# The final norm of a two-block transformer kernel: even tiles scaled on ScalarE and multiplied by the norm's weights on GpSimd, odd tiles on VectorE

## The chip, the cores and the metric

The kernel runs on one core of one Trainium2 chip. The metric is the device time of one execution in microseconds (us), as the median of several runs.

## What is computed

Two transformer blocks in float32 over 1024 tokens with 1024 features: the first has latent attention and a gated side input, the second a gated delta rule and a retention, followed by a mixture of 64 experts of which each token uses two. The change lies in the last lines of it, the sum of the two expert results of a token and the norm of the whole:

```python
def rms_norm(x, w):
    xf = x.astype(jnp.float32)
    y = xf * lax.rsqrt(jnp.mean(xf * xf, axis=-1, keepdims=True) + EPS)
    return (y * w.astype(jnp.float32)).astype(x.dtype)
...
        h2 = rms_norm(x, ffn_norm[l])
        x = x + hierarchical_moe(h2, w_router_group[l], w_router_expert[l],
                                 w_gate[l], w_up[l], w_down[l])
    return rms_norm(x, final_norm)
```

## The kernel before, in words

The program is written for each engine by hand, stage after stage, with semaphores between the engines. The tokens are cut into T = 8 tiles of 128 partitions, so a tile is 128x1024 floats (512 KB). The stages are: the projections, the attention, the output of the first block, the projections of the second block, its recurrence over tiles (the `L2042` to `L2316` lines), the experts, and the last stage, which the change touches. Nothing of the expert stage has to be known but that it leaves the two results of each token, y0 and y1, in the DRAM tensor `y_d`.

The last stage is four functions, one for each of the engines SyncE, VectorE, ScalarE and GpSimd.

- `f_sp` loads the residual tiles `xf` and the weights of the final norm `fn2` (copied to all partitions) while the experts still run, and after the last scatter loads `yf` from `y_d` in four transfers of two tiles each (L2752). Then it waits for the tiles in order, 0 to 7, and stores each to `out` (L2756). One transfer is issued as soon as its tile is done, and never ahead of a lower tile.
- `f_dve` adds in two instructions (L2767), y0 and then y1, each times its per-token weight, into `xf`. Each addition waits for its predecessor. Two tiles later it finishes the tile (`last`, L2773) with one scalar_tensor_tensor: `xf` times the per-token factor times `fn2`. It writes the tile in place.
- `f_act` squares the tile and sums the squares (L2783, an ACTIVATE and the reading of its accumulator), when y1 is in.
- `f_pool` makes the factor from the sum in two instructions on a 128x1 column: `ms` (L2788, scale and add) and `rs` (L2790, to the power -0.5). They are in order by tile.

`Count` is a helper for semaphores: each name that is "done" raises it by one, and `wait(engine, name, t)` waits until the name of tile t has been done. All are counted in the program order of one engine. Below, `rs(3)` is the L2790 instruction of tile 3, and so on; `add y0`, `add y1` are the two of L2767.

The order on VectorE is therefore add(0), add(1), add(2), last(0), add(3), last(1), and so on until add(7), last(5), last(6), last(7). Other lines that the prediction's steps name are of the recurrence stage: L2303 is a 128x1024 multiplication on GpSimd, L2042 and L2124 are 128x1024 multiplications on VectorE, L2242, L2246, L2248 are 128x512 multiplications on GpSimd, L2094 is a 128x512 addition on VectorE, L2307 is a power on GpSimd. L1018 is a Copy on ScalarE with a per-token factor over 128x1024.

Of the kernel before, what the change touches and what calls it, by code (L numbers as in the profile page):

```python
# [11 lines left out]
ALU = mybir.AluOpType  # L12
ACT = mybir.ActivationFunctionType
# [84 lines left out]
def build(nc, A, out):  # L98

    ctx = ExitStack()  # L100
    with ctx:  # L101
        def sem(name):
            return ctx.enter_context(nc.semaphore(name))
# [3 lines left out]
        def sb(name, shape, off, dt=F32):  # L107
            return nc.alloc_sbuf_tensor_at(name, shape, dt, offset=base_off + off)
# [8 lines left out]
        def wait(eng, semaphore, value):  # L117

            if not isinstance(value, int):
                eng.wait_ge(semaphore, value)
                if eng.engine in (mybir.EngineType.Pool, mybir.EngineType.SP):
                    eng.sem_inc(s_alone, 1)
            elif value > 0:
                eng.wait_ge(semaphore, value)
# [1467 lines left out]
        for s in STEPS:  # L1594
            for name in ENDING.get(s, ORDER):
                t = s - LAG[name[0]]
# [43 lines left out]
        pool_l = Count("l_pool", "ms rs"); act_l = Count("l_act", "sq"); dve_l = Count("l_dve", "hn")  # L1640
# [735 lines left out]
        def m_full(eng, b, n):  # L2376

            wait(eng, bank_full[b], n + base_m[b])
# [350 lines left out]
        xf = sb("xf", [P, T, D], SLOT[2])  # L2729
# [3 lines left out]
        fn2 = sb("fn2", [P, D], SLOT[2] + 32 * KB)  # L2733
        s_fn2 = sem("fn2_in")
        dve_f = Count("f_dve", "y0 y1", after=dve_n); dve_out = Count("f_out", "out", after=dve_a)
        act_f = Count("f_act", "sq", after=act_n)
        pool_f = Count("f_pool", "ms rs", after=pool_a)
        s_out = sem("out_stored")
        ssF, msF, rsF = ([stat_d[:, 8 * i + p:8 * i + p + 1] for p in range(4)] for i in range(3))

        def f_sp(sp):
            for q in range(2):
                wait(sp, s_x4st[q], 16 * T // 2)
            m_full(sp, 2, N_FIX - 2)
            for t in range(T):
                sp.dma_start(xf[:, t, :], x4_d[t * P:(t + 1) * P, :]).then_inc(s_xf, 16)
            m_full(sp, 5, N_FIX - 2)
            sp.dma_start(fn2[:, :], A["final_norm_2"].partition_broadcast(P)).then_inc(s_fn2, 16)
            wait(sp, s_phase, PH_M)
            for i in range(T // 2):  # L2750
                t = 2 * i
                sp.dma_start(yf[t // 4][:, t % 4:t % 4 + 2, :, :],  # L2752
                             y_d[t * 2 * P:(t + 2) * 2 * P, :].rearrange("(a p k) n -> p a k n", a=2, k=2)).then_inc(s_yf[i], 16)
            for t in range(T):
                dve_out.wait(sp, "out", t)
                sp.dma_start(out[0, t * P:(t + 1) * P, :], xf[:, t, :]).then_inc(s_out, 16)  # L2756
            wait(sp, s_out, 16 * T)

        def f_dve(v):
            v.wait_ge(s_fn2, 16)  # L2760
            v.wait_ge(s_wt, 5)
            v.wait_ge(s_xf, 16 * T)

            def add(t):
                v.wait_ge(s_yf[t // 2], 16)  # L2765
                for k in range(2):
                    dve_f.done(v.scalar_tensor_tensor(xf[:, t, :], yf[t // 4][:, t % 4, k, :], w_tok[:, k, t:t + 1], xf[:, t, :],  # L2767
                                                      ALU.mult, ALU.add), f"y{k}")
                    dve_f.wait(v, f"y{k}", t)

            def last(t):
                pool_f.wait(v, "rs", t)
                dve_out.done(v.scalar_tensor_tensor(xf[:, t, :], xf[:, t, :], rsF[t % 4], fn2[:, :], ALU.mult, ALU.mult), "out")  # L2773
            for t in range(T + 2):
                if t < T:
                    add(t)
                if t >= 2:
                    last(t - 2)

        def f_act(act):  # L2780
            for t in range(T):
                dve_f.wait(act, "y1", t)
                act_f.done(act.activation(yf[t // 4][:, t % 4, 0, :], xf[:, t, :], ACT.Square, accum_out=ssF[t % 4]), "sq")  # L2783

        def f_pool(pool):
            for t in range(T):
                act_f.wait(pool, "sq", t)
                pool_f.done(pool.tensor_scalar(msF[t % 4], ssF[t % 4], 1.0 / D, EPS, ALU.mult, ALU.add), "ms")  # L2788
                pool_f.wait(pool, "ms", t)
                pool_f.done(pool.tensor_tensor(rsF[t % 4], msF[t % 4], neghalf[:, 0:1], ALU.pow), "rs")  # L2790

        block = ctx.enter_context(nc.Block())

        @block.sync
        def _(sp):
            setup_sp(sp)
            a_sp(sp)
            att_sp(sp)
            b_sp(sp)
            c_sp(sp)  # L2800
            d0_sp(sp)
            d_sp(sp)
            moe_sp(sp)
            f_sp(sp)
# [12 lines left out]
        @block.scalar  # L2817
        def _(act):
            setup_act(act)
            a_act(act)  # L2820
            att_act(act)
            b_act(act)
            c_act(act)
            d0_act(act)
            d_act(act)
            moe_act(act)
            f_act(act)

        @block.vector
        def _(v):  # L2830
            setup_dve(v)
            a_dve(v)
            att_dve(v)
            b_dve(v)
            c_dve(v)
            d0_dve(v)
            d_dve(v)
            moe_dve(v)
            f_dve(v)

        @block.gpsimd
        def _(pool):
            a_pool(pool)
            phase_a_end(pool)
            att_pool(pool)
            b_pool(pool)
            b_end(pool)
            c_pool(pool)
            d_pool(pool)
            moe_pool(pool)  # L2850
            f_pool(pool)
# [21 lines left out]
```

## Time and profile before

| | |
|---|---|
| median of 3 runs | 2313.5 us (2313.23 to 2316.52) |
| the profiled execution, its own time | 2314.25 us |
| its span in the trace | 2312.5 us |
| VectorE busy in the whole span | 771.1 us (33%) |
| ScalarE busy | 620.4 us (27%) |
| GpSimd busy | 497.4 us (22%) |
| TensorE busy | 2029.7 us (88%) |

The trace has the time from 0 to 2312.5 us; the execution's own time has 1.75 us around it. DVE is VectorE, ACT ScalarE, POOL GpSimd, PE TensorE, SP SyncE; a letter q behind an engine is its sequencer. Busy time includes the time in which a started instruction is held by something, and this is why one and the same instruction can have different durations.

### The profile page before, as it was taken

The page shows a single profiled execution, that of the slowest core. Times are in us where ns is not written, and L with a number is a line of the kernel's source. Part 1 is how long each engine was busy: PE and PEld are TensorE (multiplying, and loading weights), DVE is VectorE, ACT ScalarE, POOL GpSimd, SP SyncE. Part 2 cuts the span into 40 slices and gives each one's busy share as a digit, 9 for nine tenths or more (in the row PEclk, how much of TensorE's full clock was granted, in tenths as well). Part 3 has the DMA queues.
Part 4 walks back from the last instruction along what each step waited for, and adds up shares of the span by engine and source line. Part 5 has one row for each costly group of instructions (what it writes and reads, how often), then busy time and mean ns, then how long its engine had stood idle before and what let it go on. Part 6 is the DMA issues. An engine that isn't in the chain of part 4 may idle for free. (4 is left out here: it accounts for less than half of the span.)

```text
span 2312.5 us, 30382 instructions
## 1 busy us (share of the span) xinstructions
PE 2029.7 (88%) x11531; PEld 1297.3 (56%) x11531; DVE 771.1 (33%) x1407; ACT 620.4 (27%) x1358; POOL 497.4 (22%) x559
## 2 busy tenths in 40 slices
PE   7999996999989999999999679989987887878780
PEld 4555553666667876687888467666653322323220
DVE  1110112555553344343111155677642111111115
ACT  2222223555542334233211243233211111111111
POOL 1122113200002111000010177656501111111103
PEclk9999997999999999999999789999987998999995
DMA  6122116212122114342232422211185999999995
GB/s 250 46 58 78 45 37 209 52 32 56 28 97 97 54 37 107 73 86 69 73 100 82 166 75 87 86 65 62 50 344 225 424 425 425 423 422 421 419 372 233
DMA packets 98423, 375.17 MB, mean 162 GB/s; under 512 B 16949, under 2 KB 33402, under 8 KB 71418
## 3 DMA queue, kind: packets, MB, share of 16 engines
q1 hardware_dynamic: 77370, 314.67, 36.7%
q0 software_dynamic: 19776, 54.55, 6.8%
q10 hardware_dynamic: 1152, 4.19, 0.4%
q8 instruction: 89, 1.46, 0.3%
q14 instruction: 36, 0.29, 0.0%
HBM read 323.04 MB, written 67.11 MB: 169 GB/s over the span
## 5 line engine op out<-in xcount | busy, mean ns | idle before, releaser
L2425 PE MATMUL ps<-w_gu,rows_t 128*64 128x512 f32 x1024 | 263.8, 675 | 63.1 <-DMA w_gu<-w_up 61.5
L2425 PEld LDWEIGHTS ps<-w_gu,rows_t 128*64 128x64 f32 x1024 | 79.9, 154 | 224.1 <-issue 158.5
L390 PE MATMUL ps<-w_u,x_t 128*128 128x512 f32 (+2 forms) x512 | 185.6, 524 | 4.3 <-DVE x_t L460 4.3
L626 PE MATMUL ps<-k_s,q_s 96*128 96x512 f32 (+3 forms) x384 | 154.5, 514 | 19.1 <-issue 19.1
L390 PEld LDWEIGHTS ps<-w_u,x_t 128*128 128x128 f32 x512 | 98.3, 192 | 90.1 <-issue 62.6
L863 PE MATMUL ps<-tk_lo,h_hi 128*128 128x512 f32 x320 | 125.5, 392 | 3.0 <-DVE tk_lo L855 3.0
L2683 POOL DMA_INDIRECT y_d<-y_out,asg_i x32 | 32.1, 1004 | 438.6 <-DVE y_out L2509 424.1
L863 PE MATMUL ps<-tk_hi,h_lo 128*128 128x512 f32 x320 | 125.1, 391 | 0.0
L863 PE MATMUL ps<-tk_hi,h_hi 128*128 128x512 f32 x320 | 125.1, 391 | 0.0
L2500 DVE TENSOR_TENSOR act_s<-act_g,ps 128x256 f32<-128x256 f32 x32 | 13.5, 421 | 334.7 <-ACT act_g L2491 334.7
L1898 PE MATMUL ps<-w_o,mix_t 128*128 128x512 f32 x256 | 124.9, 617 | 0.0
L2443 PE MATMUL ps<-w_d,act_tt 128*64 128x512 f32 x512 | 116.9, 598 | 0.5 <-issue 0.5
L755 ACT ACTIVATE prob<-ps,stats 128x256 f32<-128x256 f32 (+7 forms) x128 | 94.6, 739 | 36.6 <-DVE stats L717 35.6
L2491 ACT ACTIVATE act_g<-ps 128x256 f32<-128x256 f32 x32 | 12.3, 383 | 332.7 <-PE ps L2425 332.7
L626 PEld LDWEIGHTS ps<-k_s,q_s 96*128 96x128 f32 x384 | 64.0, 194 | 61.7 <-issue 61.2
L717 DVE TENSOR_REDUCE stats<-ps 128x1 f32<-128x256 f32 (+7 forms) x128 | 97.0, 758 | 4.7 <-DVE ps L715 0.3
L636 PEld LDWEIGHTS ps<-consts,prob 128*128 128x128 f32 x576 | 69.1, 142 | 48.7 <-issue 39.7
L636 PE MATMUL ps<-consts,prob 128*128 128x128 f32 x576 | 85.9, 276 | 11.7 <-DVE prob_t L693 10.4
L863 PE MATMUL ps<-h_lo,ch_hi 128*128 128x512 f32 x192 | 77.3, 403 | 8.9 <-DVE ch_lo L855 5.6
L650 PE MATMUL ps<-prob_t,v_all 128*64 128x128 f32 x1152 | 77.7, 280 | 1.1 <-ACT prob_t L691 0.8
L1139 POOL TENSOR_TENSOR o_s<-sz_in,rinv 128x1024 f32<-128x1024 f32 x8 | 15.8, 1977 | 288.2 <-DVE rinv L721 256.0
L863 PE MATMUL ps<-h_hi,ch_lo 128*128 128x512 f32 x192 | 76.0, 396 | 0.0
(399 smaller groups left out, 3695.9 us busy)
## 6 DMA issues: line engine op xcount, KB each, us to landing
w_gu<-w_gate SPq DMA_DIRECT2D x64, 1024.0 KB, 21.5
w_gu<-w_up SPq DMA_DIRECT2D x64, 1024.0 KB, 24.9
w_d<-w_down SPq DMA_DIRECT2D x64, 1024.0 KB, 18.9
w_tk<-w_in SPq DMA_DIRECT2D x5, 2048.0 KB, 12.1
proj_d<-tok_o POOLq DMA_DIRECT2D x40, 256.0 KB, 2.3
tk_in<-proj_d SPq DMA_DIRECT2D x8, 1280.0 KB, 5.9
yf<-y_d SPq DMA_DIRECT2D x4, 2048.0 KB, 14.4
q_d<-q_feat POOLq DMA_DIRECT2D x8, 768.0 KB, 6.6
```

Source lines behind the costliest of these rows:

```text
L390: mm = pe.matmul(b[:, 0:cn], x_t[p][:, k, :], w_u[:, k, c0:c0 + cn], start=(k == 0), stop=(k == KD - 1))
L626: mm = pe.matmul(ps[:, b, 0:cn], q_s[p][:, a, i * P:(i + 1) * P], k_s[p][:, a, g * BANK:g * BANK + cn], start=True, stop=True)
L636: mm = pe.transpose(b[:, (k - 4 * g) * P:(k - 4 * g + 1) * P], prob[j % 2][:, k * P:(k + 1) * P], ident)
L650: mm = pe.matmul(ps[half, b, (i % 4) * P:(i % 4 + 1) * P], v_all[:, k, bass.ds(u * (2 * VD) + a * VD, VD)], prob_t[(2 * i + a) % 4][:, k, ...
L717: v.tensor_reduce(nmax[j % 4], flat[:, 0:n], AX.X, ALU.max, negate=True).then_inc(s_max, 1)
L755: act.activation(prob[j % 2][:, 0:n], flat[:, 0:n], ACT.Exp, bias=nmax[j % 4], accum_out=rsum[p][:, j // 2, j % 2:j % 2 + 1]).then_inc(s_e ...
L863: mm = pe.matmul(out_, a, b_, start=(n == 0), stop=(n == 3 * len(pairs) - 1))
L1139: pool.tensor_tensor(o_s[:, :].rearrange("p (h n) -> p h n", h=HEADS), sz_in[t % 2][:, :].rearrange("p (h n) -> p h n", h=HEADS), bc(rinv[ ...
L1898: mm = pe.matmul(b, mix_t[:, k, :], w_o2[:, k, j * BANK:(j + 1) * BANK], start=(k == 0), stop=(k == KD - 1))
L2425: mm = pe.matmul(ps[half, 2, :].rearrange("p (g n) -> p g n", g=2), rows_t[:, k, half], w_gu[q][:, h, :, k, :], start=(k == 0), stop=(k == ...
L2443: mm = pe.matmul(ps[half, 4 + j, :], act_tt[:, k, half], w_d[q][:, h, k, j * BANK:(j + 1) * BANK], start=(k == 0), stop=(k == 1))
L2683: pool.indirect_dma_start(out=y_d, out_offset=bass.IndirectOffsetOnAxis(ap=idx, axis=0), in_=y_out[q][:, :], in_offset=None, bounds_check= ...
```

## The change

In the last stage the finishing of the even tiles 0, 2, 4 and 6 is taken from VectorE. ScalarE multiplies the tile by its per-token factor, in place, in the iteration of the next odd tile and ahead of that tile's square. GpSimd multiplies it by `fn2`, in place, behind `rs` of the next odd tile. SyncE waits for GpSimd or VectorE by the parity of the tile. GpSimd also waits once for the load of `fn2`. The odd tiles are finished on VectorE at the place where they were.

```diff
+        act_s2 = Count("f_act_scaled", "scaled", after=act_l); pool_out = Count("f_pool_out", "out", after=pool_l)
...
             for t in range(T):
-                dve_out.wait(sp, "out", t)
+                (dve_out if t % 2 else pool_out).wait(sp, "out", t // 2)
                 sp.dma_start(out[0, t * P:(t + 1) * P, :], xf[:, t, :]).then_inc(s_out, 16)
...
             for t in range(T + 2):
                 if t < T:
                     add(t)
-                if t >= 2:
+                if t >= 2 and t % 2:
                     last(t - 2)
 
         def f_act(act):
+            def scaled(t):
+                pool_f.wait(act, "rs", t)
+                act_s2.done(act.activation(xf[:, t, :], xf[:, t, :], ACT.Copy, scale=rsF[t % 4]), "scaled")
+
             for t in range(T):
+                if t % 2:
+                    scaled(t - 1)
                 dve_f.wait(act, "y1", t)
                 act_f.done(act.activation(yf[t // 4][:, t % 4, 0, :], xf[:, t, :], ACT.Square, accum_out=ssF[t % 4]), "sq")
 
         def f_pool(pool):
+            pool.wait_ge(s_fn2, 16)
             for t in range(T):
                 act_f.wait(pool, "sq", t)
                 pool_f.done(pool.tensor_scalar(msF[t % 4], ssF[t % 4], 1.0 / D, EPS, ALU.mult, ALU.add), "ms")
                 pool_f.wait(pool, "ms", t)
                 pool_f.done(pool.tensor_tensor(rsF[t % 4], msF[t % 4], neghalf[:, 0:1], ALU.pow), "rs")
+                if t % 2:
+                    act_s2.wait(pool, "scaled", t // 2)
+                    pool_out.done(pool.tensor_tensor(xf[:, t - 1, :], xf[:, t - 1, :], fn2[:, :], ALU.mult), "out")
```

## Rows read from the trace of the kernel before

**Rows 1.** The page: the span, and the lines of the chain that ended last

```profile
span 2312.5 us, 30382 instructions
...
DVE xf L2767 1%; DMA yf<-y_d 0%; DVE xf L2773 0%; POOL stat_d L2788 0%; ACT yf L2783 0%; DMA y_d<-y_out,asg_i 0%; POOLq L2385 0%; POOLq L101 0%; ACTq L101 0%; POOLq L2386 0%; DVEq L2765 0%; POOLq L2725 0%
```

**Rows 2.** The chain that ended last, in order of time: start, us, what

```profile
2273.36 1.30 DVE xf L2767
...
2285.12 1.28 DVE xf L2773
2286.41 1.21 DVE xf L2767
...
2300.47 1.06 ACT yf L2783
...
2303.66 1.28 DVE xf L2773
```

**Rows 3.** Groups by line and form from 2270 us on: busy us, mean ns, idle before

```profile
L2767 DVE SCALAR_TENSOR_TENSOR xf<-yf,w_tok,xf 128x1024 f32<-128x1024 f32 x16 | 20.5, 1283 | 12.9 <-DMA yf<-y_d 12.5
...
L2773 DVE SCALAR_TENSOR_TENSOR xf<-xf,stat_d,fn 128x1024 f32<-128x1024 f32 x8 | 10.2, 1284 | 0.9 <-POOL stat_d L2790 0.7
L2783 ACT ACTIVATE yf<-xf 128x1024 f32<-128x1024 f32 x8 | 8.5, 1057 | 33.4 <-DVE xf L2767 33.4
...
L2783 ACT ACTIVATION_READ_ACCUMULATOR yf<-xf 128x1 f32 x8 | 1.5, 187 | 0.0
```

**Rows 4.** Timeline of the last stage: start, us, instruction, idle before it

```profile
2277.25 0.19 POOL L2788 TENSOR_SCALAR stat_d<-stat_d 128x1 f32<-128x1 f32 x1 [14.58 <-ACT yf L2783]
2277.52 1.52 POOL L2790 TENSOR_TENSOR stat_d<-stat_d,consts 128x1 f32<-128x1 f32 x1
...
2282.49 2.60 DVE L2767 SCALAR_TENSOR_TENSOR xf<-yf,w_tok,xf 128x1024 f32<-128x1024 f32 x2
2282.52 1.30 POOL L2788 TENSOR_SCALAR stat_d<-stat_d 128x1 f32<-128x1 f32 x1 [0.86 <-ACT yf L2783]
...
2283.90 1.59 POOL L2790 TENSOR_TENSOR stat_d<-stat_d,consts 128x1 f32<-128x1 f32 x1
...
2303.09 0.54 POOL L2790 TENSOR_TENSOR stat_d<-stat_d,consts 128x1 f32<-128x1 f32 x1
```

**Rows 5.** Groups by line and form, whole span: nearest rows for both added instructions

```profile
L1018 ACT ACTIVATE h_tok<-res,stats 128x1024 f32<-128x1024 f32 x8 | 9.2, 1154 | 7.7 <-POOL stats L493 7.7
...
L2303 POOL TENSOR_TENSOR mixed<-o_cat,tk_in 128x1024 f32<-128x1024 f32 x8 | 18.8, 2350 | 19.7 <-DVE o_cat L2115 19.2
```

**Rows 6.** Timeline of the recurrence stage, 1383 to 1392 us

```profile
1383.71 2.35 POOL L2303 TENSOR_TENSOR mixed<-o_cat,tk_in 128x1024 f32<-128x1024 f32 x1
...
1384.12 3.02 DVE L2042 TENSOR_TENSOR qk_n<-qkv_in,stat_d 128x1024 f32<-128x1024 f32 x1
...
1387.28 1.67 POOL L2307 TENSOR_TENSOR stat_d<-stat_d,consts 128x8 f32<-128x8 f32 x1
...
1388.92 1.03 POOL L2242 TENSOR_TENSOR tri_g<-consts,gates 128x512 f32<-128x512 f32 x1
1388.98 2.05 DVE L2124 TENSOR_TENSOR mixed<-mixed,stat_d 128x1024 f32<-128x1024 f32 x1 [1.51 <-POOL stat_d L2307]
```

**Rows 7.** Timeline of the recurrence stage, 1360 to 1364 us, GpSimd and VectorE

```profile
1360.56 1.04 POOL L2246 TENSOR_TENSOR d_low<-d_low,gates 128x512 f32<-128x512 f32 x1 [4.33 <-ACT d_low L1966]
1361.56 1.72 POOL L2248 TENSOR_TENSOR d_up<-d_up,consts 128x512 f32<-128x512 f32 x1
...
1360.92 1.22 DVE L2094 TENSOR_TENSOR rhs<-rhs,v_b 128x512 f32<-128x512 f32 x1
```

**Rows 8.** Transfers: the last store (issue, landing) and the last two loads of yf

```profile
2304.98 0.33 SPq L2756 DMA_DIRECT2D out<-xf  x1
...
out<-xf SPq DMA_DIRECT2D x1, 512.0 KB, 2.6
...
DMA to landing us min/median/max: 16.6/19.2/21.8
```

## The prediction, as it was made before the changed kernel ran

> **What bounds the kernel now.** I read the chain that ended last first, because the change lies in the last stage alone, and what counts there is what the end waits for. The page gives the lines [rows 1]: of the last stage mostly L2767, the additions on VectorE. In order of time [rows 2] the chain is the addition of tile 0 at 2273.36, then VectorE instruction after instruction until the last addition is in at 2300.45, then the square of tile 7 on ScalarE (2300.47), its two small GpSimd instructions, and last(7) on VectorE, 2303.66 to 2304.94. Groups by line second [rows 3]: 24 VectorE instructions of 1.28 us, 30.7 of the 31.6 us from the first to the last; idle inside is 0.7 us. So VectorE is the bound of this stage, and it is 1.4% of the span. The earlier stages are not touched, and I take them as the same. After last(7) comes its store, issued at 2304.98, landing 2.6 us later [rows 8], and some 4.9 us of ending that no instruction of the change touches (2312.5 less 2307.6).
>
> Third, the timeline of the stage [rows 4], for what the groups hide. `ms` takes 0.19 us when it meets no VectorE instruction, but 1.30 us at 2282.52: it ends at 2283.82, just behind the end of an addition that the row at 2282.49 puts at about 2283.78. `rs` takes 0.54 us when VectorE is idle (2303.09), but 1.59 us at 2283.90, ending 0.39 us after the addition that ends at 2285.10. GpSimd waits for the running VectorE instruction to end. VectorE shows nothing of it here, all 24 have 1.28 us.
>
> **The change, part by part.** *Removed:* last(0), (2), (4), (6) on VectorE. A `last` adds 1.2 us to the row of additions: with the addition behind it it takes 1.28 + 1.21 on the chain, where an addition alone takes 1.30 [rows 2]; the two overlap a little. Three of the four stood ahead of the last addition (the fourth stood in the shadow of tile 7's square), so at most 3 x 1.2 = 3.6 us go from the path there.
>
> *Added on ScalarE:* four Copy with a per-token factor, 1.15 us each by L1018 [rows 5]. ScalarE idles 33 us in the stage [rows 3], so its load costs nothing; its place does. scaled(t-1) stands ahead of the square of tile t and waits for rs(t-1). So sq(t), ms(t), rs(t) and last(t) of the odd tiles now stand behind rs(t-1), 1.15 us and the queue of GpSimd.
>
> *Added on GpSimd:* four 128x1024 multiplications, 2.35 us each alone by L2303 [rows 5]. They stand behind rs of the odd tile, and ahead of ms and rs of the next even tile. The wait for `scaled` costs nothing: by then ScalarE has done also the following square. The wait for fn2 costs nothing: VectorE waited for the same load before its first addition, four us before GpSimd's first `ms`.
>
> *What a big GpSimd instruction costs VectorE* is the term that decides. The last stage shows only small ones, and from them the price is 0. In the recurrence stage a big one stands beside it [rows 6]: L2303 runs 1383.71 to 1386.06, L2042 starts at 1384.12 and ends at 1387.14, 1.08 us after the other's end; alone such an instruction takes 1.22 to 1.28. So it was held for the whole of it. The other way round [rows 7]: L2248, started at 1361.56, ends at 1363.28, 1.14 us after L2094 has ended (1362.14), which itself had waited until L2246 ended. Each holds the other and the waiting one is let in next. Bounds: 0 (small ones) and 1.98 us for each multiplication (2.20 after VectorE's end, plus 1.08, less 1.30). I take the upper, since the rows with the same size of instruction and two inputs from SBUF on VectorE are L2042 and L2124; all 20 remaining VectorE instructions have two such inputs.
>
> The Trainium skill (SBUF — State Buffer, section Who interferes with whom) says that a VectorE instruction with two SBUF inputs and a GpSimd instruction that reads SBUF exclude each other for the whole instruction, and that the order of issue decides who is blocked. With it the sum is the one below; without it, the one of the first rival.
>
> *Who is first.* When `rs` of an odd tile ends, both the multiplication and, if VectorE already waits, `last` can start. At 1388.95 exactly this happened [rows 6]: L2307 ended, L2242 behind it on GpSimd started at 1388.92, L2124, which waited for L2307, at 1388.98; L2242 kept its 1.03 us and L2124 ended 1.08 us after it. So GpSimd goes first.
>
> *Now the times.* Until add y1 of tile 1 (2278.62) and rs(0) (ends 2279.04 [rows 4]) all is as before. scaled(0) 2279.07 to 2280.22. Square and accumulator of tile 1, 1.16 us from start to end [rows 3], as the two overlap by 0.09 and starting 0.09 before the Copy ends: until 2281.29. ms(1) starts at 2281.38, is held by the addition that ends at 2282.56, ends 2282.60; rs(1) from 2282.68 is held by the addition until 2283.88 and ends 2284.27. VectorE has no last(0) any more, has finished add(3), and waits 0.4 us for rs(1). out(0), the multiplication, starts at 2284.23.
>
> From one multiplication's start to the next the chain is: multiplication 2.35; last(1), held, ends 1.08 later, and ms(2), held by it, 0.04 after that; rs(2) is held by the next addition, 1.21 + 0.39 after last(1), so 1.56 more; scaled(2) 0.03 + 1.15; square 1.07; 0.09 to ms(3), which an addition holds until 1.24 after its start; 0.08, and rs(3) with VectorE idle again, 0.54, less 0.04 overlap: 9.2 us for two tiles. Before, a tile took its two additions and a last, 2.60 [rows 4] + 1.2 and the gaps, 3.84, and two tiles 7.7. VectorE's own work in it (four additions, one last, one multiplication to wait for) is some 8.5, and it fits. So out(2) starts at 2293.4, out(4) at 2302.6. The last round has no more additions to hold rs(6) and ms(7): 9.2 less 0.94 and less 1.05 is 7.2, out(6) starts at 2309.8 and ends at 2312.2. last(7), held behind it, ends at 2313.3. The loads of yf don't matter: the last landed at 2266.9 + 21.8 = 2288.7 [rows 8], its addition starts at about 2296.8.
>
> *Stores.* SP waits for tile 6 and then 7. out(6) is done 1.1 us before last(7), the issue takes 0.33 [rows 8], and a store needs about 1.3 us of transfer (my estimate: half of the 2.6 us to its landing): the end follows last(7) as before. All told the end goes from 2304.94 to 2313.3: **8.3 us later**. Against the profiled execution's own 2314.25 this is 2322.6; that execution was 0.75 above the median, so for the median 2313.5 + 8.3 = 2321.8 us, 0.36% slower. Some 0.2% (4.6 us) is what a measurement of this kernel can tell from no change.
>
> **Rivals.** *1. Nothing holds VectorE, the multiplications run beside it* (the small ones in rows 4 speak for it, rows 6 against it). Additions end at 2300.45 - 3.6 = 2296.8; y1 of tile 6 is in two additions earlier, 2294.2, and 1.27 to ms(6) (as 2275.98 to 2277.25 for tile 0), 0.27 and 0.54 later rs(6) is done, 2296.3; then scaled(6) until 2297.4, square, ms(7) and rs(7) until 2299.4, out(6) until 2301.7. 3.2 us earlier, and the store of tile 7, behind that of tile 6, gives back up to 1.2: 2310.3 to 2311.5 us. That is not slower, and within 0.2%. It decides as soon as a multiplication costs VectorE less than about 1 us. 10%.
>
> *2. VectorE goes first at each rs* (against it the one case of rows 6; for it that GpSimd has one more wait in its queue here, at which a small pair of instructions leaves 0.08 us, while VectorE starts 0.03 us after rs). Then last runs its 1.28, and the multiplication ends 2.20 after it. ms of the odd tile is free in return, the period is 9.4, and out(6) ends at 2314.2, with the store of tile 7 still to be issued behind it, 1.2 later: 10.4 us, 2323.9 us. 20%.
>
> *3. VectorE keeps its place through a row of instructions and the multiplication gets in only when VectorE idles.* Five instructions, 6.5 us, would go ahead of each multiplication and the chain behind it: some 17 us, 2330 us. Against it: GpSimd's small ones get in at each end of a VectorE instruction, and rows 7. 3%.
>
> *4. The change saves as intended* by over 0.2%: even without any hold the tail gives 3.2 us; more would need a multiplication much under 2.35, which no row has. 3%.
>
> **How the numbers follow.** The forecast case has 62%; in it each of the near ties (who is held at ms(1), a hold more or less in a round) is worth up to 1.2 us either way, and the runs' own scatter upwards is 3 us. The range 2317.5 to 2326 takes in this case and the second rival, and leaves out the first, third and fourth and a bit of the scatter. Slower by over 0.2% (above 2318.1): forecast, rivals 2 and 3, 0.85; within: rival 1 and what is left, 0.12; faster 0.03.
>
> **What the changed profile would show.** VectorE's instructions: 20, of which four or five take 2 to 3.3 us in place of 1.28, each ending 1.08 us after a GpSimd multiplication. The multiplications 2.35 us each, starting some 9.2 us apart, the first near 2284.2. VectorE idle before last(3), (5) by `rs`, and some 3.8 us before last(7). ScalarE's scaled instructions waiting for rs(t-1). The last VectorE instruction ends near 2313.3. I am wrong if the multiplications leave the additions at 1.28 us (rival 1), if they take 3.5 us after an rs while `last` has 1.28 (rival 2), or if the Copy on ScalarE takes much over 1.15.

## The result, and the profile after

The changed kernel takes 2320.6 us (median of 15 runs, 2316.05 to 2324.2) against 2313.2 us before (15 runs, 2310.93 to 2316.52). The ratio is 1.003, with a 95% interval of 1.0022 to 1.0038: slower by 7.4 us, where 8.3 were forecast. The profiled execution took 2321.51 us; its span is 2319.8.

The stages ahead of the last one vary by a few us from run to run, so I compare one length, read from the trace: the **stage**, from the start of the first addition to the end of the last VectorE or GpSimd instruction. Before it was 2273.36 to 2304.94, 31.58 us [rows 2]. After it is 2272.53 to 2311.97, 39.44 us: 7.86 us more, and the first addition was 0.83 us earlier. Each such length is read from one profiled execution.

The stage's end is not what the time follows. At the end of the program the engines have a DRAIN (L101), and GpSimd's is the last to finish. The rows give its duration in ns and its start in us, first before, then after the change:

```profile
L101 POOLq DRAIN  x1: 9261/9261/9261, 2303.0 to 2303.0; - x1
...
L101 SPq DRAIN  x1: 7/7/7, 2307.7 to 2307.7; - x1
```

```profile
L101 POOLq DRAIN  x1: 11564/11564/11564, 2308.0 to 2308.0; - x1
...
L101 SPq DRAIN  x1: 7/7/7, 2314.9 to 2314.9; - x1
```

SyncE waits for all stores to land before its DRAIN, so they are in at 2307.7 and 2314.9; GpSimd's DRAIN ends only at 2312.31 and 2319.56. In all eleven traces of this document the span ends 8.90 to 8.92 us after the end of GpSimd's last computing instruction, while from VectorE's last one it is 6.1 to 11.1 us, and SyncE's DRAIN is 2.9 to 4.8 us ahead of the end of GpSimd's. So there is a second length, **to GpSimd's end**, from the start of the first addition to the end of GpSimd's last computing instruction: 30.27 us before (`rs(7)` ends at 2303.63), 38.35 us after (the multiplication of tile 6 ends at 2310.88). It is 8.08 us longer, and this is the one that the time follows.

The groups by line and form of the last stage after the change (busy us, mean ns, then the idle time before them and what ended it), to be read beside [rows 3]:

```profile
L2768 DVE SCALAR_TENSOR_TENSOR xf<-yf,w_tok,xf 128x1024 f32<-128x1024 f32 x16 | 20.6, 1285 | 12.6 <-DMA yf<-y_d 12.1
L2774 DVE SCALAR_TENSOR_TENSOR xf<-xf,stat_d,fn 128x1024 f32<-128x1024 f32 x4 | 13.2, 3305 | 5.3 <-POOL stat_d L2798 5.3
L2798 POOL TENSOR_TENSOR stat_d<-stat_d,consts 128x1 f32<-128x1 f32 x8 | 9.8, 1228 | 0.7
L2801 POOL TENSOR_TENSOR xf<-xf,fn 128x1024 f32<-128x1024 f32 x4 | 9.3, 2328 | 0.0
...
L2796 POOL TENSOR_SCALAR stat_d<-stat_d 128x1 f32<-128x1 f32 x8 | 5.2, 648 | 23.8 <-ACT yf L2790 23.5
L2784 ACT ACTIVATE xf<-xf,stat_d 128x1024 f32<-128x1024 f32 x4 | 4.6, 1148 | 19.3 <-POOL stat_d L2798 19.3
```

VectorE has 20 instructions in place of 24, but the four `last` take 3.3 us each, where all had 1.28. VectorE now also idles 5.3 us before them, where before it idled 0.7. The multiplications take 2.33 us, the Copy 1.15, as the nearest rows said [rows 5].

Below, a **handover** is the moment at which `rs` of an odd tile ends and both the multiplication and `last` can start, and the **period** is the time from one multiplication's start to the next. One round of two tiles in the timeline of the changed kernel (start, us, instruction):

```profile
2283.45 2.33 POOL L2801 TENSOR_TENSOR xf<-xf,fn 128x1024 f32<-128x1024 f32 x1
2283.58 3.29 DVE L2774 SCALAR_TENSOR_TENSOR xf<-xf,stat_d,fn 128x1024 f32<-128x1024 f32 x1 [0.51 <-POOL stat_d L2798]
...
2285.87 1.05 POOL L2796 TENSOR_SCALAR stat_d<-stat_d 128x1 f32<-128x1 f32 x1
2286.79 5.24 DVE L2768 SCALAR_TENSOR_TENSOR xf<-yf,w_tok,xf 128x1024 f32<-128x1024 f32 x4
2287.00 1.46 POOL L2798 TENSOR_TENSOR stat_d<-stat_d,consts 128x1 f32<-128x1 f32 x1
2288.50 1.15 ACT L2784 ACTIVATE xf<-xf,stat_d 128x1024 f32<-128x1024 f32 x1 [6.89 <-POOL stat_d L2798]
...
2290.77 0.19 POOL L2796 TENSOR_SCALAR stat_d<-stat_d 128x1 f32<-128x1 f32 x1 [2.31 <-ACT yf L2790]
2291.05 1.39 POOL L2798 TENSOR_TENSOR stat_d<-stat_d,consts 128x1 f32<-128x1 f32 x1
...
2292.41 2.33 POOL L2801 TENSOR_TENSOR xf<-xf,fn 128x1024 f32<-128x1024 f32 x1
2292.54 3.29 DVE L2774 SCALAR_TENSOR_TENSOR xf<-xf,stat_d,fn 128x1024 f32<-128x1024 f32 x1 [0.50 <-POOL stat_d L2798]
```

The multiplication of tile 0 (L2801) starts at 2283.45 and ends at 2285.78. `last(1)` starts 0.13 us behind it and ends at 2286.87, 1.09 us after the multiplication. `ms(2)` is held by `last(1)` and ends 0.05 us after it, `rs(2)` is held by the next addition. Only then can ScalarE scale tile 2 (2288.50), and only behind this stands the square of tile 3, whose sum `rs(3)` needs (2291.05). The next multiplication starts at 2292.41, 8.96 us after the first.

The chain that ended last, as the profile follows it back, is no longer a row of additions but goes through all three engines (start, us, what):

```profile
2283.48 2.31 POOL xf L2801
...
2287.00 1.47 POOL stat_d L2798
...
2288.50 1.15 ACT xf L2784
2289.65 1.05 ACT yf L2790 x2
...
2292.43 2.31 POOL xf L2801
...
2308.61 3.36 DVE xf L2774
```

And who waited for whom in the stage (us in total, times, longest):

```profile
POOL stat_d L2796 <- ACT yf L2790: 23.5, 5, 14.3
ACT xf L2784 <- POOL stat_d L2798: 19.3, 4, 6.9
...
DVE xf L2774 <- POOL stat_d L2798: 5.3, 4, 3.8
```

ScalarE waits 19.3 us for `rs`; before, it waited for nothing but the additions. GpSimd in turn waits for the squares, 9.2 us beyond the 14.3 ahead of its first instruction, and VectorE 5.3 us for `rs`: each waits for another, and the chain goes round.

### The profile page after: what moved, and what is told of

Same layout as the page of the kernel before. It is cut to its first block and busy times, and to the rows that moved or that the text cites. A ratio compares the mean times of both kernels' runs of the same rounds, so it can differ in the third digit from the quotient of the medians.

```text
span 2319.8 us, 30387 instructions
## 1 busy us (share of the span) xinstructions
PE 2029.8 (88%) x11531; PEld 1297.4 (56%) x11531; DVE 772.6 (33%) x1403; ACT 624.2 (27%) x1362; POOL 502.5 (22%) x563
## 6 DMA issues: line engine op xcount, KB each, us to landing
yf<-y_d SPq DMA_DIRECT2D x4, 2048.0 KB, 14.3
```

## Experiments

The experiments were made to split the 7.86 us: the order on ScalarE, the time in GpSimd's queue, and the port. By the **port** I mean only what the rows show: that a VectorE instruction with two inputs in SBUF and a GpSimd instruction that reads SBUF hold each other. "Rival" in the expectations is always the other explanation. All stages are read as above, each from one trace; the length to GpSimd's end stands beside them where it tells something else. Runs e1 to e5 and e8 are one execution each, and as the time of one execution scatters by some us their times are not compared; e6, e7 and e9 have 11. All diffs are against the changed kernel unless said otherwise.

**e1: the multiplications left out.** The even tiles come out without the norm's weights.

```diff
-                    act_s2.wait(pool, "scaled", t // 2)
-                    pool_out.done(pool.tensor_tensor(xf[:, t - 1, :], xf[:, t - 1, :], fn2[:, :], ALU.mult), "out")
...
-                (dve_out if t % 2 else pool_out).wait(sp, "out", t // 2)
+                dve_out.wait(sp, "out", t // 2) if t % 2 else act_s2.wait(sp, "scaled", t // 2)
```

> The multiplications by the norm's weights on GpSimd are left out (even tiles are only scaled, so their output lacks the weights); the order on ScalarE stays. I call the stage the time from the start of the first addition to the end of the last VectorE or GpSimd instruction: 31.6 us before, 39.4 us after the change. Port theory (a GpSimd multiplication and a VectorE instruction exclude each other, and the multiplication also stands in GpSimd's queue): without it the stage falls to about 31.5 us. What stays above the 26 us of VectorE's own work is the chain rs(t-1), scaled(t-1), square(t). The four finishing instructions on VectorE take 1.28 us each. Rival (the cost is the chain over ScalarE alone): then most of it stays, 37 us or more.

Measured: the stage is 31.05 us (2269.58 to 2300.63), and each `last` takes 1.28 us. So the 8.4 us between this and 39.44 come with the multiplication (8.6 us to GpSimd's end, 29.74 against 38.35). But it is also only 0.5 us shorter than before the change, although VectorE has four instructions less: something else eats these.

**e8: ScalarE's order, without multiplications.** The edit above and this one (the weights are missing here too):

```diff
-                if t % 2:
-                    scaled(t - 1)
                 dve_f.wait(act, "y1", t)
                 act_f.done(act.activation(yf[t // 4][:, t % 4, 0, :], xf[:, t, :], ACT.Square, accum_out=ssF[t % 4]), "sq")
+                if t % 2:
+                    scaled(t - 1)
```

> As e1 (no multiplications on GpSimd, even tiles lack the weights), and with scaled(t-1) behind the square of tile t. Nothing of the change is left but that VectorE has four instructions less. Expected by the row of VectorE: last addition at 23.4 us, then last(5), and last(7) ends at 26.7 to 27.0 us of stage, 4.7 us less than before the change. Against e1's 31.05 it says what ScalarE's order costs, about 4.2 us. Rival (the order costs nothing where GpSimd is free): 31 us again.

Measured: 26.89 us (2273.68 to 2300.57). This is what four VectorE instructions less are worth where they leave nothing behind: 4.7 us. The place of `scaled` ahead of the square costs 31.05 less 26.89, 4.2 us. Both differences are the same to GpSimd's end (25.57 us here). The waits of VectorE for `rs` show where: the `last` rows of both kernels, first with `scaled` ahead (mean ns, idle before), then with it behind.

```profile
L2774 DVE SCALAR_TENSOR_TENSOR xf<-xf,stat_d,fn 128x1024 f32<-128x1024 f32 x4 | 5.1, 1284 | 5.1 <-POOL stat_d L2798 5.1
```

```profile
L2774 DVE SCALAR_TENSOR_TENSOR xf<-xf,stat_d,fn 128x1024 f32<-128x1024 f32 x4 | 5.1, 1285 | 0.9 <-POOL stat_d L2798 0.8
```

**e2: GpSimd busy for about the same time, but reading nothing.** The multiplication gives way to a filling with zeros, so the even tiles again lack the weights.

```diff
+        spare = sb("spare", [P, 2600], SLOT[2] + 36 * KB)
...
-                    pool_out.done(pool.tensor_tensor(xf[:, t - 1, :], xf[:, t - 1, :], fn2[:, :], ALU.mult), "out")
+                    pool_out.done(pool.memset(spare[:, :], 0.0), "out")
```

> Each multiplication on GpSimd is replaced, at the same place in its queue and for about the same 2.33 us, by filling a spare buffer with zeros, which reads nothing (the even tiles lack the weights). Port theory: last(1), (3), (5), (7) take 1.28 us and no longer 3.3, ms and rs behind the filling are held only by VectorE, the period of two tiles falls from 8.96 to some 7.4 us and the stage from 39.4 to 34.4 us: 5.0 us are the port, the rest of the 7.9 is the queue. Rival (only the queue and the chain count, the port adds nothing): the stage stays at 39.4. If writing also takes the port, last keeps 3.3 us.

Measured: 34.25 us (2272.39 to 2306.64). The timeline of one handover:

```profile
2283.29 2.25 POOL L2802 MEMSET spare<- 128x2600 f32 x1
2283.44 1.28 DVE L2775 SCALAR_TENSOR_TENSOR xf<-xf,stat_d,fn 128x1024 f32<-128x1024 f32 x1 [0.51 <-POOL stat_d L2799]
2284.64 5.24 DVE L2769 SCALAR_TENSOR_TENSOR xf<-yf,w_tok,xf 128x1024 f32<-128x1024 f32 x4
...
2285.63 0.34 POOL L2797 TENSOR_SCALAR stat_d<-stat_d 128x1 f32<-128x1 f32 x1
```

The filling of 2.25 us runs from 2283.29 to 2285.54, and `last(1)` beside it has 1.28 us. The additions behind it are not held either: four take 5.24 us. So in the stage 2.25 us in GpSimd's queue cost 34.25 less 31.05, 3.2 us, and the reads of the multiplication the other 5.2. To GpSimd's end, which the time follows, the split is another: 34.25 less 29.74, 4.5 us for the queue, and 38.35 less 34.25, 4.1 us for the reads (some 0.3 of it because four fillings are 0.08 us shorter each). The difference is at the end: the last filling, after `rs(7)`, lengthens the time by its whole 2.25 us, although it writes nothing that is needed. The rival, that the port adds nothing, falls by either length.

**e3: the port alone, in the kernel before.** Against the kernel before, GpSimd also waits for `fn2` at its start, and:

```diff
                 pool_f.done(pool.tensor_tensor(rsF[t % 4], msF[t % 4], neghalf[:, 0:1], ALU.pow), "rs")
+                if t % 2:
+                    pool.tensor_tensor(spare[:, 0:D], fn2[:, :], fn2[:, :], ALU.mult)
```

> The kernel before, with one edit: GpSimd also does a 128x1024 multiplication of two SBUF operands into a spare buffer after rs of each odd tile. Nobody waits for it, and VectorE keeps its 24 instructions. Port theory: each of the four holds VectorE by about 2.0 us, the stage goes from 31.6 to about 39.5 us, as long as after the change although no engine waits for the result. Rival (the chain over ScalarE is the cost): 31.6 to 33 us.

Measured: 38.11 us (2272.17 to 2310.28), 6.53 more than before, from four instructions for whose result nobody waits.

```profile
2280.09 1.28 DVE L2774 SCALAR_TENSOR_TENSOR xf<-xf,stat_d,fn 128x1024 f32<-128x1024 f32 x1
2280.44 2.68 POOL L2794 TENSOR_TENSOR spare<-fn 128x1024 f32<-128x1024 f32 x1
...
2281.30 4.24 DVE L2768 SCALAR_TENSOR_TENSOR xf<-yf,w_tok,xf 128x1024 f32<-128x1024 f32 x2
...
2307.31 1.88 POOL L2794 TENSOR_TENSOR spare<-fn 128x1024 f32<-128x1024 f32 x1
2307.37 2.91 DVE L2774 SCALAR_TENSOR_TENSOR xf<-xf,stat_d,fn 128x1024 f32<-128x1024 f32 x1 [0.71 <-POOL stat_d L2792]
```

The multiplication at 2280.44 is held by `last(0)` until 2281.37 and ends at 2283.12; the two additions from 2281.30 take 4.24 in place of 2.60 us, 1.64 more. Four times 1.63 is the 6.53. I had expected about 2.0 each (1.98 in the prediction), where the multiplication was to end 2.20 us after VectorE's instruction. It ended 1.75 us after it: this multiplication, of `fn2` by itself, takes 1.88 us (2307.31), not 2.33. The mechanism is as expected, and the shorter GpSimd instruction accounts for the smaller size. To GpSimd's end it is 37.03 us, 6.76 more than before: three holds, and the 1.88 us of the last multiplication itself, which comes after `rs(7)`.

**e4: `scaled` behind the square, with multiplications.** Only the second edit above, that of e8.

> The changed kernel with scaled(t-1) behind the square of tile t on ScalarE, so that the square no longer waits for rs(t-1). Port theory: VectorE's 20 instructions and four holds are the bound then, some 8.6 us for two tiles; by hand I get a stage of 35.3 us, ending with the multiplication of tile 6. The order of ScalarE's queue is then worth 4 us of the 7.9. Rival (the port holds are all of the loss): the stage stays within 1 us of 39.4, since the holds are the same.

Measured: 35.49 us (2271.73 to 2307.22), the multiplication of tile 6 being the last. Groups:

```profile
L2768 DVE SCALAR_TENSOR_TENSOR xf<-yf,w_tok,xf 128x1024 f32<-128x1024 f32 x16 | 26.4, 1652 | 12.6 <-DMA yf<-y_d 12.2
L2801 POOL TENSOR_TENSOR xf<-xf,fn 128x1024 f32<-128x1024 f32 x4 | 12.6, 3141 | 0.4 <-ACT xf L2784 0.4
...
L2774 DVE SCALAR_TENSOR_TENSOR xf<-xf,stat_d,fn 128x1024 f32<-128x1024 f32 x4 | 5.1, 1285 | 1.4 <-POOL stat_d L2798 1.3
```

Here `last` has 1.28 us, but the additions have 1.65 on average and the multiplications 3.14: now the two hold each other at other places. Three of the four times a multiplication starts while an addition runs, and the fourth while `last(7)` runs; the first, at 2280.01, ends 2.20 us after the addition that holds it, the figure that the prediction had for this. The order of ScalarE's queue is worth 4 us of the stage, but 2.9 us to GpSimd's end (35.49 for 38.35), as `last(7)` no longer comes last. It does not make the change a gain: this is still 5.2 above the 30.27 before.

**e5: `last` with one SBUF input.** ScalarE copies the weights once to PSUM, ahead of the stage, and `last` reads them there.

```diff
+            act.activation(fps, fn2[:, :], ACT.Copy).then_inc(s_fps, 1)
...
-                dve_out.done(v.scalar_tensor_tensor(xf[:, t, :], xf[:, t, :], rsF[t % 4], fn2[:, :], ALU.mult, ALU.mult), "out")
+                dve_out.done(v.scalar_tensor_tensor(xf[:, t, :], xf[:, t, :], rsF[t % 4], fps, ALU.mult, ALU.mult), "out")
```

`fps` is two banks of PSUM. 

> The changed kernel; ScalarE copies the norm's weights once to PSUM ahead of the stage, and VectorE's last reads them there, so that last has one SBUF input (the additions keep two). Port theory: last(1), (3), (5), (7) take about 1.3 us beside the multiplication in place of 3.3, and the first addition behind each is held instead, so the period of two tiles stays at 9.0. Only the end is shorter: it becomes the end of the multiplication of tile 6, about 1.0 us earlier, stage 38.4 us. Rival (a GpSimd multiplication holds every VectorE instruction, whatever it reads): last keeps 3.3 us and the stage 39.4.

Measured: 36.08 us (2268.97 to 2305.05).

```profile
2279.89 2.33 POOL L2807 TENSOR_TENSOR xf<-xf,fn 128x1024 f32<-128x1024 f32 x1
2280.02 1.28 DVE L2777 SCALAR_TENSOR_TENSOR xf<-xf,stat_d,ps 128x1024 f32<-128x1024 f32 x1 [0.52 <-POOL stat_d L2804]
2281.22 6.06 DVE L2771 SCALAR_TENSOR_TENSOR xf<-yf,w_tok,xf 128x1024 f32<-128x1024 f32 x4
...
2287.62 0.54 POOL L2804 TENSOR_TENSOR stat_d<-stat_d,consts 128x1 f32<-128x1 f32 x1
...
2288.14 2.34 POOL L2807 TENSOR_TENSOR xf<-xf,fn 128x1024 f32<-128x1024 f32 x1
```

`last(1)` takes 1.28 us in the middle of the multiplication, and the additions behind it 6.06 in place of 5.24: the one with two SBUF inputs is held, the one with a PSUM input is not. That part stands. The period does not: 8.25 us (2279.89 to 2288.14), where I had expected 9.0. VectorE's additions end at 2287.28, 0.06 us ahead of `ms(3)` (2287.34), so that neither `ms(3)` nor `rs(3)` is held (0.19 and 0.54 us), where in the changed kernel `rs(3)` took 1.39. With `last` out of the way the additions end 7.4 us after the multiplication's start, not 8.6 as in the changed kernel, and these 1.2 us removed a hold of 0.85. To GpSimd's end it is 36.08 for 38.35, 2.3 us less, all of it in the three periods.

**e6 and e7: no VectorE instruction with two SBUF inputs.** ScalarE puts y0 times its weight into PSUM (`acc`, three buffers), VectorE works from there, and four tiles (0 to 3) go to GpSimd in e6, five in e7. Of the edit of e6, the main lines:

```diff
+                act.activation(acc(t), yf[t // 4][:, t % 4, 0, :], ACT.Copy, scale=w_tok[:, 0, t:t + 1]).then_inc(s_m0, 1)
...
+                dve_f.done(v.tensor_tensor(acc(t), acc(t), xf[:, t, :], ALU.add), "y0")
+                dve_f.wait(v, "y0", t)
+                dve_f.done(v.scalar_tensor_tensor(xf[:, t, :], yf[t // 4][:, t % 4, 1, :], w_tok[:, 1, t:t + 1], acc(t),
+                                                  ALU.mult, ALU.add), "y1")
...
-                if t >= 2 and t % 2:
+                if t - 2 >= 4:
                     last(t - 2)
```

> No VectorE instruction of the stage has two SBUF inputs: ScalarE writes y0 times its weight to PSUM, VectorE adds the residual there, then adds y1 times its weight into SBUF, and reads the norm's weights from PSUM. Squares stand ahead of all else on ScalarE. Tiles 0 to 3 are scaled on ScalarE and multiplied on GpSimd, tiles 4 to 7 finished on VectorE. Port theory: all 20 VectorE instructions take about 1.3 us, the multiplications 2.33, ms 0.19, rs 0.54; the stage takes 26 to 27 us, 5 us less than before, so about 0.2% faster than before. Rival (GpSimd holds VectorE whatever it reads): VectorE's instructions of up to 3.3 us, the stage over 33 us.

> As e6, with tile 4 also taken from VectorE (19 VectorE instructions, five multiplications on GpSimd). Port theory: VectorE has 1.2 us less before the last addition, but rs(6) and rs(7) stand behind the fifth multiplication and a longer queue on ScalarE: 26 us, within 1 us of e6 either way. Rival: over 35 us.

Measured with four tiles: 28.09 us of stage (2272.18 to 2300.27), and 0.9985 of the time before (95%: 0.9976 to 0.9994). With five: 29.49 us, 0.9994 (0.9985 to 1.0003), no difference that can be told; this is 3.5 us over the 26 expected and 1.4 over the stage with four, where I had allowed 1. Groups with four tiles:

```profile
L2774 DVE SCALAR_TENSOR_TENSOR xf<-yf,w_tok,ps 128x1024 f32<-128x1024 f32 x8 | 10.2, 1281 | 0.3
L2772 DVE TENSOR_TENSOR ps<-ps,xf 128x1024 f32<-128x1024 f32 x8 | 9.9, 1232 | 14.1 <-ACT ps L2794 13.9
...
L2780 DVE SCALAR_TENSOR_TENSOR xf<-xf,stat_d,ps 128x1024 f32<-128x1024 f32 x4 | 4.9, 1277 | 2.1 <-POOL stat_d L2816 2.0
...
L2816 POOL TENSOR_TENSOR stat_d<-stat_d,consts 128x1 f32<-128x1 f32 x8 | 4.3, 542 | 0.7
L2814 POOL TENSOR_SCALAR stat_d<-stat_d 128x1 f32<-128x1 f32 x8 | 1.5, 190 | 20.1 <-ACT yf L2804 19.7
```

No engine holds another any more: every VectorE instruction has its 1.23 or 1.28 us, the multiplications 2.35, `ms` 0.19 and `rs` 0.54 for all eight tiles. This is the clearest sign for the port: with one input of each VectorE instruction in PSUM the holds are gone. The stage is still 1 to 2 us over what I had expected, for a wait that I had not reckoned with: last(4) stands ahead of the additions of tile 6 and waited 2.0 us for rs(4) behind a multiplication. With five tiles VectorE waits 4.0 us for `rs`. A second wait lies ahead of the stage as I count it: the first addition (2272.18) waits for ScalarE's product, which starts at 2270.94 and delays it by some 1.1 us (in e9, where the two don't wait for each other, they start 0.1 us apart). Together with the length to GpSimd's end, 26.47 us with four tiles and 27.88 with five, this makes the gain some 2.6 and 1.2 us, by my estimate, and both lie in the intervals of the times.

**e9: the same in another order**, with the first addition on VectorE as before, `scaled` ahead of the next product, and all four `last` behind all additions:

```diff
-            for t in range(T + 2):
-                if t < T:
-                    add(t)
-                if t - 2 >= 4:
-                    last(t - 2)
+            for t in range(T):
+                add(t)
+            for t in range(4, T):
+                last(t)
```

> As e6 with three changes of order, made against what its trace showed: the first addition is VectorE's own again (in e6 it waited for ScalarE's product), scaled stands ahead of the next product on ScalarE, and last(4) to (7) stand behind all additions (in e6 last(4) waited 2.0 us for rs(4) ahead of the additions of tile 6 and 7). Port theory: additions back to back, 16 times 1.3 is 20.9 us, last(4), (5), (6) 3.7 us beside the square and rs of tile 7, last(7) ends at 25.9 us of stage, 5.7 less than before: some 0.25% faster than before. If GpSimd's queue (four multiplications of 2.35 and eight pairs of ms and rs of 0.8 us, 16 us in all) is late, rs(7) sets the end at up to 27 us. Rival (VectorE is held whatever it reads): over 33 us. If the gain in the stage does not reach the time, the loads and stores around it would have to be longer than the 7.5 us from the last instruction to the end before.

Measured: 28.03 us (2273.22 to 2301.25), and 0.9974 of the time before (0.9965 to 0.9983): it beats both kernels. VectorE and ScalarE in its groups:

```profile
L2776 DVE TENSOR_TENSOR ps<-ps,xf 128x1024 f32<-128x1024 f32 x7 | 8.6, 1233 | 2.7 <-ACT ps L2797 2.6
...
L2784 DVE SCALAR_TENSOR_TENSOR xf<-xf,stat_d,ps 128x1024 f32<-128x1024 f32 x4 | 4.9, 1276 | 0.0
L2793 ACT ACTIVATE xf<-xf,stat_d 128x1024 f32<-128x1024 f32 x4 | 4.5, 1132 | 0.0
```

The wait for `rs` is gone, but VectorE waits 2.6 us for ScalarE's products (L2776). ScalarE has a square, a scaling and a product for each of the tiles 1 to 4, 3.1 us, where VectorE needs 2.6 for its two additions: I had counted ScalarE's total and not its load in the stretch where all three fall together. So the 25.9 us were not reached, nor the 27 that I had given as the most. The time fell by 5.5 us in the medians (3.9 to 8.1 by the interval), the stage by only 3.55, and from its last instruction to the end of the span are 6.15 us, where before there were 7.56. The length to GpSimd's end accounts for this: 25.21 us (`rs(7)` ends at 2298.43), 5.06 less than before, and from there to the end of the span 8.92 us as before. With the four `last` behind all additions none stands on the way to `rs(7)`, and the last two of them start after GpSimd's last instruction, where they cost nothing.

## Why the prediction was right

**The bound and the sum.** The time was 2320.6 where 2321.8 was forecast, and slower by over 0.2%, as the larger part of the chances had it. The stage was to end 8.3 us later; it is longer by 7.86. Two of the terms on which it rested stand: a multiplication holds VectorE until its end, and the odd tiles' square stands behind scaled and rs of the even tile.

**One step was wrong, and luck kept the number right.** "The end follows last(7) as before" does not hold, nor did it before the change. The end follows GpSimd's last instruction by 8.92 us in both kernels, and what the prediction took for the ending of the store, "some 4.9 us", is GpSimd's DRAIN. By the prediction's own times this would have made the multiplication of tile 6, 2312.2, less `rs(7)` before, 2303.63: 8.6 us in place of 8.3. The two lie so near because `last(7)` ends 1.31 us after GpSimd before the change and 1.09 us after it in the changed kernel. Measured to GpSimd's end it is 8.08.

The runs without and with each term give the sum in full, where the prediction had it only as a chain:

| step | run | stage us | to GpSimd's end us | difference of the latter |
|---|---|---|---|---|
| before | before | 31.58 | 30.27 | |
| four VectorE instructions less, `scaled` where it holds up nothing | e8 | 26.89 | 25.57 | -4.7 |
| scaled ahead of the square | e1 | 31.05 | 29.74 | +4.2 |
| 2.25 us more in GpSimd's queue for each pair | e2 | 34.25 | 34.25 | +4.5 |
| that instruction reads SBUF, as VectorE does | after | 39.44 | 38.35 | +4.1 |

So the port is one of three terms of about the same size: without it the changed kernel would still be 4.0 us over the one before. The terms depend on this order of taking them; from the other side, the better order on ScalarE saves 2.9 us with the multiplications in place (e4).

**Step by step.** *Removed:* at most 3.6 us from the row ahead of the last addition, forecast; 4.7 measured for the whole stage. The difference is in the tail: before, ms(7) began beside the second of two `last` and was held for 1.1 us, and in e8 the one `last` there ends as ms(7) begins, which takes 0.19 us. I had put the fourth `last` down as hidden; it was not. *ScalarE:* 1.15 us, right; that its place matters, right. *GpSimd:* 2.35, measured 2.33. *The price on VectorE:* end of the multiplication plus 1.08, measured 1.09. *Who is first:* GpSimd, at all four handovers; at the first three its instruction started 0.13 us ahead of `last`, at the last one 0.06. *The period:* 9.2 forecast, 8.96 measured. The part that was off is "ms(3), which an addition holds until 1.24 after its start": it started 0.03 us after the addition and got through in 0.19, and rs(3) was held instead, 1.39 for the 0.54 I had. The prediction had it start 0.09 after the addition; such ties I had priced at up to 1.2 us, and this was worth some 0.2 a round. *The last round:* 7.2 forecast, 7.18 measured. *The stores:* they cost nothing in any run, as SyncE is through with them 2.9 us or more ahead of GpSimd's DRAIN. The 1.2 us that the first two rivals had for the store of tile 7 are shown nowhere: where both last stores were issued close together (e2, e4, e5) the span ended 8.92 us after GpSimd's last instruction, as elsewhere.

**The rivals.** The first, that the multiplications run beside VectorE unhindered, falls with the 3.3 us of `last`; the filling (e2) and the weights in PSUM (e5) show what it takes to make it true. The second, VectorE first, did not happen at any of the four handovers. The third, that VectorE keeps its place through a row, is refuted by the 9 us period, and in e4 the multiplication gets in behind the one instruction that runs. The fourth, a saving, is refuted by the ratio. The rule of the Trainium skill (SBUF — State Buffer, section Who interferes with whom) agrees with these runs: an instruction with two SBUF inputs is held by one that reads (3.3 us), and not by one that only writes (1.28 us).

What stays open is why GpSimd is first at each handover: no run changes who is first. Why GpSimd's DRAIN takes as long as it does no run shows either.

## What to carry to other kernels

Before work is moved from VectorE to GpSimd, look at the inputs of what stays on VectorE: with two operands in SBUF each large multiplication on GpSimd costs VectorE nearly its whole length, here 2 us for 1.3 saved (the 128x1 ones cost it nothing). One operand in PSUM removes this. An instruction moved to an idle engine costs by its place in that engine's queue: ahead of a step that the next tile needs it put 4 us on the path, behind it next to nothing. And look at what the end of the program waits for: in these traces the program ends a fixed 8.9 us after GpSimd's last instruction, while VectorE's last instruction and the stores have some us to spare.

## What was not expected of the hardware

From the end of GpSimd's last computing instruction to the end of the span are 8.90 to 8.92 us in all eleven traces, whatever VectorE and the stores do meanwhile.

A multiplication on GpSimd of a 128x1024 tensor by itself took 1.88 us, of two different tensors 2.33 to 2.35; why is not shown.

And `ms` can pass just behind the start of a VectorE instruction. In the changed kernel `ms(3)`, 0.03 us behind the start of an addition, took 0.19 us, and `ms(1)`, 0.06 us behind one, took 1.27. Before the change `ms(2)` took 1.30 though it started only 0.03 us behind an addition; there `last(0)`, the VectorE instruction ahead of that addition, still ran until 2282.57. Small shifts on one engine so move the holds on the other, up to 0.85 us at a time in these runs.
